# Seven block products in a second output layer, their order and sums rearranged, and a fourth buffer for arriving weights

## The reference, cut to what matters

```python
def conv_ffn(x, w_up, conv_w, conv_b, w_down):
    u = causal_dwconv(x @ w_up, conv_w, conv_b)
    g, val = jnp.split(u, 2, axis=-1)
    return (jax.nn.gelu(g) * val) @ w_down          # 512 x 2816 times 2816 x 1024
...
    m = jnp.square(jax.nn.relu(h @ mlp_w1[l])) @ mlp_w2[l]   # 512 x 4096 times 4096 x 1024
    x = x + rms_norm(m, post_mlp_g[l])              # the end of the kernel
```

## Time and profile before

| | us |
|---|---|
| median of 3 runs (lowest, highest) | 1262.27 (1262.15, 1262.39) |
| the profiled execution, whole | 1265.27 |
| its span, from first to last instruction | 1263.4 |
| PE busy | 1246.5 |
| DVE busy | 816.8 |
| ACT busy | 608.2 |

### The profile page before, as it was taken

One profiled execution on the slowest core, in us unless ns is written; L12 is line 12 of the kernel. 1 busy time (PEld: TensorE's weight loads), 2 busy tenths in 40 slices (PEclk: granted clock), 3 DMA queues, 4 the chain that ended last, 5 costly groups with the idle time before them and its releaser, 6 DMA issues.

```text
span 1263.4 us, 16035 instructions
## 1 busy us (share of the span) xinstructions
PE 1246.5 (99%) x6278; PEld 1047.0 (83%) x6278; DVE 816.8 (65%) x1179; ACT 608.2 (48%) x1022; POOL 28.9 (2%) x40
## 2 busy tenths in 40 slices
PE   9999999999999999999999999999999999899997
PEld 9877798898888888888888898778898888788785
DVE  5778878575577555555633488888574443577785
ACT  4565654254446444444522364578443422365563
POOL 0000001000000000000000000000000000000000
PEclk9999999999999999999999999999999999999999
DMA  8345445422236466545754276434473333256562
GB/s 265 136 150 200 134 134 183 145 73 67 84 118 200 167 167 156 167 163 148 209 166 164 78 176 196 134 106 149 130 200 100 101 100 99 101 183 200 166 202 98
DMA packets 53892, 186.79 MB, mean 148 GB/s; under 512 B 5781, under 2 KB 13461, under 8 KB 49465
## 3 DMA queue, kind: packets, MB, share of 16 engines
q1 hardware_dynamic: 48776, 151.82, 37.1%
q0 software_dynamic: 4608, 33.56, 10.7%
q10 hardware_dynamic: 432, 0.39, 0.1%
HBM read 177.88 MB, written 39.32 MB: 172 GB/s over the span
## 4 chain that ended last, share of the span: by engine, by line
PE 84%; DVE 3%; ACT 2%; issue 1%; DVEq 0%; ACTq 0%
PE bank L1392 16%; PE bank L1393 15%; PE bank L1394 15%; PE bank L1593 3%; PE bank L1594 3%; PE bank L1595 3%; PE bank L1533 3%; PE bank L1538 3%; PE bank L1535 3%; PE bank L1536 3%; PE bank L1534 3%; PE bank L1537 3%; PE bank L1643 1%; DVE wlo L2318 1%; PE bank L1514 1%
## 5 line engine op out<-in xcount | busy, mean ns | idle before, releaser
L1392 PE MATMUL bank<-xh,whi 128*128 128x512 f32 (+1 forms) x1136 | 413.7, 364 | 1.0 <-DVE R L2553 0.8
L1393 PE MATMUL bank<-xl,whi 128*128 128x512 f32 (+1 forms) x1136 | 409.9, 361 | 0.0
L1394 PE MATMUL bank<-xh,wlo 128*128 128x512 f32 (+1 forms) x1136 | 409.8, 361 | 0.0
L2318 DVE TENSOR_TENSOR wlo<-stage,whi 128x1024 fp32r<-128x1024 f32 (+1 forms) x246 | 296.7, 1211 | 156.2 <-ACT whi L1826 154.8
L1826 ACT CAST whi<-stage 128x1024 fp32r<-128x1024 f32 (+1 forms) x246 | 254.0, 1038 | 130.7 <-PE bank L1538 58.6
L1392 PEld LDWEIGHTS bank<-xh,whi 128*128 128x128 f32 x1136 | 214.4, 189 | 38.8 <-issue 5.5
L1394 PEld LDWEIGHTS bank<-xh,wlo 128*128 128x128 f32 x1136 | 214.4, 189 | 32.8
L1393 PEld LDWEIGHTS bank<-xl,whi 128*128 128x128 f32 x1136 | 214.5, 189 | 31.8 <-issue 0.2
L1593 PE MATMUL bank<-whi,xh 128*128 128x512 f32 x220 | 86.4, 393 | 5.6 <-issue 3.2
L1595 PE MATMUL bank<-whi,xl 128*128 128x512 f32 x220 | 86.3, 392 | 0.0
L1594 PE MATMUL bank<-wlo,xh 128*128 128x512 f32 x220 | 86.3, 392 | 0.0
(11 more groups left out here) (374 smaller groups left out, 1625.2 us busy)
## 6 DMA issues: line engine op xcount, KB each, us to landing
stage<-in_W_m SPq DMA_DIRECT2D x56, 512.0 KB, 3.6
stage<-in_W_up SPq DMA_DIRECT2D x44, 512.0 KB, 3.7
stage<-in_W_down SPq DMA_DIRECT2D x22, 512.0 KB, 3.6
stage<-in_W_in_a SPq DMA_DIRECT2D x19, 512.0 KB, 3.8
stage<-in_W_out SPq DMA_DIRECT2D x16, 512.0 KB, 4.1
sum_a<-in_W_m POOLq DMA_DIRECT2D x8, 1024.0 KB, 8.0
sum_b<-in_W_m POOLq DMA_DIRECT2D x8, 1024.0 KB, 7.4
stage<-in_W_in_b SPq DMA_DIRECT2D x10, 512.0 KB, 4.2
```

The costliest lines, as they stand in the source:

```text
L1392: e.matmul(b[:, cols], hi[:, k, :], xh[:, k, cols], start=(k == 0), stop=False)
L1393: e.matmul(b[:, cols], hi[:, k, :], xl[:, k, cols], start=False, stop=False)
L1394: last = e.matmul(b[:, cols], lo[:, k, :], xh[:, k, cols], start=False, stop=(k == 7))
L2318: e.tensor_tensor(wlo[:, plan.place[i], c], stage[:, i % NSTAGE, c], whi[:, plan.place[i], c].bitcast(F32), ALU.subtract).then_inc(S["w_lo"])
```

## The change

- **down** is now computed like m2 for the first 16 of its 22 tiles of hidden width: 4 groups, 28 products of 12 matmuls each (16 in part one, 12 in part two), and then the 6 remaining tiles as full chunks as before. The layer has 34 chunks instead of 22. The six full chunks are exactly the six that its tail takes tile by tile.
- Sums and combinations carry the layer's name (down_a to down_d, m2_a to m2_d). There are 48 DMAs on GpSimd instead of 32, one for every two chunks: 22 of them during up, none during down, the rest from the first chunk of the second mixer to chunk 23 of m1.
- The last chunk of up and of m1 signals a semaphore (half) after its first 12 matmuls. The tiles x_from 1 to 3 of the layer that follows wait for that and stand in front of the last chunk's own evaluation.
- In both layers the combination r2 of group 0 is made early, beside the first tile. In m2 the combinations r1 and r3 of group 7 are moved behind x_from 4 to 6.
- Around the change of parts: pump (the split of a chunk) now stands in front of taken; the x_from that stood there and in the next two steps come together after c21. 
- Part two takes t22, t12, r4 for every group but the first.
- ScalarE's squares of the last layer go to sq2 instead of sq, and its waits for pn_x are gone there.
- NSTAGE is 4, with the room taken from the tile more (4 tiles instead of 6; two of the r tiles of m2 now lie in gb). Two semaphores were merged to stay within their number.

The core of the diff:

```diff
-NSTAGE, NSPLIT = 3, 6
+NSTAGE, NSPLIT = 4, 6
...
-           ("xq", 8), ("xo", 8), ("up", 44), ("down", 22), ("in2_c", 4), ("in2_a", 2), ("in2_v", 2), ("in2_d", 2), ("in2_b", 10),
+           ("xq", 8), ("xo", 8), ("up", 44), ("down", 34), ("in2_c", 4), ("in2_a", 2), ("in2_v", 2), ("in2_d", 2), ("in2_b", 10),
...
-SEVEN = ([(kind, g) for g in range(8) for kind in ("r1", "r2", "t11", "r3")]
-         + [(kind, g) for g in range(8) for kind in ("t12", "r4", "t22")])
+GROUPS = {"down": 4, "m2": 8}
+SEVEN = {n: [(kind, g) for g in range(k) for kind in ("r1", "r2", "t11", "r3")]
+         + [(kind, g) for g in range(k) for kind in (("t22", "t12", "r4") if g else ("t12", "r4", "t22"))]
+         for n, k in GROUPS.items()}
+LAST_X = {"down": ("up", 2 * NF1 - 1), "m2": ("m1", NF2 - 1)}
...
         for j in self.feat("up", 2 * NF1):
+            if j == 2 * NF1 - 1:
+                self.seven_ahead("down")
             self.step("up", j // 2, j % 2)
             self.out(("up", j), "up_y", j + 1)
+            if j % 8 == 7 and j < 8 * GROUPS["down"]:
+                self.combine("down", "r1", j // 8)
+                self.combine("down", "r3", j // 8)
...
-        self.tok_full("down", NF1)
+        self.seven("down")
...
+    def seven_ahead(self, name):
+        for i in range(1, 4):
+            self.seven_x(name, i)
...
         for i in range(n - 6):
             self.need()
-            self.step("seven", i)
+            self.step("seven", name, i)
             self.used += 1
-            if i == 29:
-                self.step("taken")
-            if i == 30:
+            ready = [i + 7]
+            if i == last - 2:
+                ready = []
+                self.pump()
+                self.step("taken", name)
+            elif i == last - 1:
+                ready = []
                 for kind in ("v", "w"):
                     for t in range(2):
-                        self.combine(kind, t)
-            if i == 31:
-                self.step("seed")
+                        self.combine(name, kind, t)
+            elif i == last:
+                ready = [i + 5, i + 6, i + 7]
+                self.step("seed", name)
                 for kind in ("c22", "c21"):
                     for t in range(2):
-                        self.combine(kind, t)
+                        self.combine(name, kind, t)
             self.pump()
-            if i + 7 < n:
-                x_from(i + 7)
+            for k in ready:
+                if k < n:
+                    self.seven_x(name, k)
...
+                if (name, j) in LAST_X.values():
+                    by_weights(b, i, cols, range(4)).then_inc(S["half"])
+                    ks = range(4, 8)
...
             def last_norm():
...
-                q.wait_ge(S["pn_x"], 7)
...
-                    e.activation(sq[:, hf * 512:(hf + 1) * 512], bank_of("m2", 2 * t + hf)[:], ACT.Square,
+                    e.activation(sq2[:, hf * 512:(hf + 1) * 512], bank_of("m2", 2 * t + hf)[:], ACT.Square,
```

More of the change, by code:

```diff
@@ new lines, in seven_x, with seven_first, seven @@
+    def seven_x(self, name, i):
+        kind, g = SEVEN[name][i] if i < len(SEVEN[name]) else ("", 0)
+        if kind in ("r2", "r4") and i > 1:
+            self.combine(name, kind, g)
+        self.step("x_from", name, i)
+        self.x_split(name, i)
+    def seven_first(self, name):
+        self.step("first", name)
+        self.combine(name, "r2", 0)
+    def seven_ahead(self, name):
+        for i in range(1, 4):
+            self.seven_x(name, i)
+    def seven(self, name):
+        n, last = NK[name], 4 * GROUPS[name] - 1
@@ L1064, in seven @@
         for kind in ("r1", "r2", "t11", "r3"):
             for b in INTO[kind]:
-                self.fill("m2", b)
-        for i in range(1, 7):
-            x_from(i)
+                self.fill(name, b)
+        for i in range(4, 7):
+            self.seven_x(name, i)
+        if name == "m2":
+            self.combine("m2", "r1", 7)
+            self.combine("m2", "r3", 7)
         for i in range(n - 6):
             self.need()
-            self.step("seven", i)
+            self.step("seven", name, i)
@@ L1101, in mlp @@
         self.step("rows", "pl")
-        self.seven()
+        self.seven("m2")
         self.step("warm", 4)
@@ L1143 @@
 SEMAPHORES = (
-    ["st0", "st1", "st2"] + [f"ld_x{k}" for k in range(5)]
+    ["st0", "st1", "st2", "st3"] + [f"ld_x{k}" for k in range(5)]
     + ["ld_w0", "ld_xf", "w0_lo", "ld_xr", "ld_c", "ld_masks", "ld_bias", "ld_mem", "ld_rows",
@@ L1292, in build_program, with t_of, seven_x @@
         hid2 = tiles(reg(16, NF2 * 512), NF2)
-        rs = [tiles(more[:, g, :], 2) for g in range(6)] + [tiles(reg(92 + 2 * g, 512), 2) for g in range(2)]
+        rs = ([tiles(more[:, g, :], 2) for g in range(4)] + [tiles(reg(92 + 2 * g, 512), 2) for g in range(2)]
+              + [tiles(gb[:, 1, 512 * g:512 * g + 512], 2) for g in range(2)])
+        hidden = {"down": hid1, "m2": hid2}
         vs, ws = tiles(sq, 2), tiles(sq2, 2)
-        def t_of(which, g):
+        def t_of(name, which, g):
             i, j = int(which[1]) - 1, int(which[2]) - 1
-            return hid2[:, 4 * g + 2 * j:4 * g + 2 * j + 2, 256 * i:256 * i + 256]
-        def seven_x(i):
-            kind, g = SEVEN[i]
+            return hidden[name][:, 4 * g + 2 * j:4 * g + 2 * j + 2, 256 * i:256 * i + 256]
+        def seven_x(name, i):
+            kind, g = SEVEN[name][i]
             if kind == "r3":
-                return t_of("t21", g)
-            return t_of(kind, g) if kind[0] == "t" else rs[g]
+                return t_of(name, "t21", g)
+            return t_of(name, kind, g) if kind[0] == "t" else rs[g]
         source = {"out1": hT, "down": hid1, "out2": yT, "m2": hid2}
@@ L1591, in seven_products @@
                     c = slice(256 * j + 128 * t, 256 * j + 128 * t + 128)
-                    new, end = i < 4 and j == 0, g == 7 and j == 1
+                    new, end = i < 4 and j == 0, g == GROUPS[name] - 1 and j == 1
                     e.matmul(b[:], x[:, c], hi, start=new, stop=False, skip_group_check=True)
@@ L1848, in x_from @@
             def x_from(name, k):
-                q.wait_ge(S["mm"], CHUNK0[name] + max(0, k - 7))
+                if name in SEVEN and k < 4:
+                    q.wait_ge(S["half"], HALVES[name])
+                else:
+                    q.wait_ge(S["mm"], CHUNK0[name] + max(0, k - 7))
                 if name == "out1":
```

238 lines of the change are left out of this document (123 added, 115 removed).

## The result

The changed kernel takes 1241.96 us (median of four runs, 1241.44 to 1243.73) against 1262.33 for the kernel before in the same series (1262.15 to 1264.06). The ratio is 0.9838 (0.9821 to 0.9855), the medians are 20.4 us apart. The forecast was 20.5 off and 1241.8.

The account below looks back on a forecast made before the run. PE, busy 99% of the span, was taken to bound the kernel. Terms of 10.9 + 0.3 + 4.9 + 1.3 + 3.1 = 20.5 us took the median from 1262.27 to 1241.8, range 1238.8 to 1247.5.

Parts of the forecast that it names:

- 48 matmuls and the start of down: Down: 48 fewer matmuls at 0.226 us give 10.9 us, and the hole at its start goes, 0.3 us.
- start of m2: Start of m2: the hole goes, 3.3 us, and the clock no longer falls, 1.6 us; together 4.9 us.
- change of parts in m2: Between parts one and two of m2: PE's idle time behind v goes, 1.3 us.
- tail of m2: Tail of m2: the wait behind the last wlo goes by earlier t22 chunks, 1.2 us.
- the end: Last tile: ScalarE's squares no longer wait for VectorE; 3.1 us together with the tail's hole of 1.2.
- transfers, fourth buffer: Whole kernel: chunks and sums land in time, 0, with at most 1 us for late loads; a fourth buffer may save 0.5.
- Down has no hole of its own at the change: Down's change of parts: 0 forecast; rival, new holes in down or a rest of m2's, 1243 to 1248, chance 0.19.
- over 8: Down: a chunk's landing would have to rise from 3.6 us to over 8 for transfers to turn the sign.
- The rival that transfers starve the products: Up and down: crowded sums make chunks land late and stretch every product, for example 1279 us; slower, chance 0.03.
- the 3.0 us between profile and median of before: Whole kernel: the gap between profiled execution, 1265.27, and median, 1262.27, was assumed to stay the same.

Follow-up runs that it names:

- experiment 1: The changed kernel with down as 22 full chunks again, without its sums and early tiles: 1253.58 us, ratio 0.9924.
- experiment 9: The changed kernel with ScalarE's squares of the last layer in sq again and its waits for VectorE back: 1244.0 us, ratio 0.9851.
- experiment 10: The changed kernel with three buffers (NSTAGE 3) in place of four: 1242.04 us, ratio 0.9836.
- experiment 4: The changed kernel with the old change of parts in both layers, taken before the split and no x_from put off: 1246.62 us, ratio 0.987.
- experiment 5: The changed kernel with x_from in their old place at the change of parts, the split still before taken: 1245.15 us, ratio 0.9863.
- experiment 8: The changed kernel with the old change of parts and the old order of kinds together, in both layers: 1247.37 us, ratio 0.9882.
- Experiment 11: The changed kernel, four buffers, with m2's sums 22 to 47 started in down, one per chunk: 1248.61 us, ratio 0.9887.
- experiment 12: The changed kernel with m2's sums 22 to 47 started in down, and three buffers instead of four: 1261.04 us, ratio 0.9986.
- experiment 2: The changed kernel with tiles 1 to 3 of down and m2 no longer made before the preceding layer's last chunk is evaluated: 1247.70 us, ratio 0.9877.
- experiment 7: The changed kernel with part two as t12, r4, t22 in every group: 1243.78 us, ratio 0.9847.

## Why the prediction was right

Its terms beside what the runs showed:

| term | forecast | measured |
|---|---|---|
| 48 matmuls and the start of down | 10.9 + 0.3 | 11.24 in the traces, 11.6 by experiment 1 |
| start of m2 | 4.9 | 3.34 + 1.67 = 5.0 in the trace of before |
| change of parts in m2 | 1.3 | 1.42 + 0.09 = 1.5 |
| tail of m2 | 1.2 | 1.32 + 0.13 = 1.45 |
| the end | 1.9 | 1.87; 2.0 by experiment 9 |
| transfers, fourth buffer | 0 | 0 (experiment 10) |
| sum | 20.5 | 21.2 in the traces (0.1 of it in no term above), 20.4 between the medians |

- **The matmuls.** 48 x 0.226 us held: the whole of down is 11.24 shorter, 10.88 of it at 0.2267 each and 0.36 the hole at its start. The figure of 131 ns that I set beside it from the Trainium skill ("TensorE: Matmul & The Clock Gate", section "Back-to-back issue gap") would have made an estimated 6.3 us. The trace of after does not agree: of its 4391 matmuls of 128 by 512 columns all but one start 0.22 us or more before the next.
- **The start of down.** The hole went, by a shorter way than laid out: ScalarE began to cast tiles 1 to 3 0.8 us before the end of up (612.87) and not 2.7, because a cast of weights (611.93) stood in front. VectorE was through with them 1.2, 1.8 and 2.4 us behind the end, about as forecast (1 to 2.2), and PE needed the first at 2.7.
- **The start of m2.** Right in kind and size, hole and clock. The forecast read the clock's part from one hole of before, which happened to be at the small end: across all runs a hole of 3 to 4.4 us cost 1.67 to 2.9 us on top.
- **The change of parts.** The schedule laid out step by step is the part I trusted least, and it can be laid beside the rows. Product 29 is over at about 1163.4. Counted from there v was to be done at 4.0, w at 5.3, the seeds at 5.9, c21 at 9.0. The rows say 4.1, 5.3, 6.0 and 8.9. The size 1.3 was the row's idle time before the instruction; what counts is the distance of starts and the two matmuls behind it, and that was 1.5. The same holds for the tail (1.2 against 1.45). Both errors are in the same direction and come to 0.45 us.
- **Down has no hole of its own at the change.** That rival had most of the rest. Experiments 4, 5 and 8 show what stood behind it: without the putting-off the hole is there, 1.3 to 1.8 us in each layer, so it was a live case. Its place is right and its releaser was not: with the new kinds it is a seed.
- **The end.** VectorE was forecast to be through with the third tile 0.5 us before PE ends; the rows say 1233.73 against 1234.21. The squares now follow PE. Behind them VectorE's L2945 ends at 1235.65 and ScalarE's root at 1235.49, so an earlier root alone would bring nothing. To let VectorE read the last bank beside ScalarE's square might, and that wasn't tried.
- **Transfers.** The 0 was right. The working behind it was too easy. I took 10.9 us as what a chunk has for landing and split, and "over 8" as the landing from which it hurts. Experiment 11 makes holes with a median landing of 6.0 us. A median says little: chunks read from sums took up to 9.4 and one wait was 8.0 us. The rival that transfers starve the products was named with the right mechanism (the section "Issuing engines are not separate DMA queues" of "DMA: Bandwidth & Descriptors" in the Trainium skill, that GpSimd's DMAs run on the same 16 as SyncE's; experiments 11 and 12 agree: SyncE's chunks went from 4.1 us to 6.0 and 6.4). To come true it needed more than this change does: the sums that after leaves to the second mixer, crowded into down.

Two things in the forecast were right by luck. The first is how close it came: by the traces the change is worth 21.2 us, 0.7 more than the terms, and the ratio of the medians leaves 18 to 23, so a forecast of 20.5 against 20.4 is closer than the working was. The second: I let the 3.0 us between profile and median of before stand on both sides. They did not: after's profiled execution lies 0.4 below its median, at 1241.57 where the working gave 1244.8, and the stretch before up is 2.4 us shorter in it than in before's. The forecast was made for the median, so it changed nothing.

## What to carry over

Read each engine's queue in order and give every step the moment at which PE needs it. At m2's change of parts that gave four moments to within 0.1 us. The experiments then showed which moves were needed (tiles made ahead, x_from put off) and which was not (the split before taken). Cost a hole by the distance of starts, not by the idle time in the row, and put 1.5 to 3 us on top for the clock when it is about 3 us or more (behind 1.8 us or less the clock stayed up, and no hole between the two was seen). Give a buffer its worth only at the load it is for: the fourth was worth 0 in this kernel, and 12 us when the same sums started in down and not in the second mixer.

## What the runs showed of the hardware

- **Slow stretches behind holes.** In the two output layers a hole of 1.8 us or less never lowered the granted clock (eleven holes of 1.0 to 1.8 us in experiments 2, 4, 5, 7, 8 and in before). Each of seven of 2.95 us or more did. What was lost after it, in us, by size of hole: 2.95: 1.67; 3.34: 1.67; 3.40: 2.73; 3.82: 2.65; 4.01: 2.93; 4.37: 2.53; 9.30: 1.44. It does not follow the hole's size. It does follow the stretch of low clock: by the record of the granted clock that lasts 3.4 us behind the holes of 2.95 and 3.34, where it begins 0.85 and 1.1 us after PE has resumed, and 6.8 us at the other five, where it begins inside the hole. What is lost is, to within 0.1 us, half of the part in which PE works again, which comes in the same order to 1.71, 1.71, 2.84, 2.74, 3.04, 2.61 and 1.46. So the hole of 9.30 loses least: 3.9 of its 6.8 us at 1.2 GHz passed while PE stood. One of the short ones, from experiment 2:

```profile
620.89:624.30 3.41, 3.41 (x10) 2.64 (x9) 2.73 (x5) 1.92 (x3) 0.00 (x0) 0.50 0.80 300
```

  What PE did before each hole was the same dense work at 1.00. What sets the start and the length of the low stretch is open.
- **Late handovers.** An instruction of VectorE normally starts 0.10 us after the ScalarE instruction that it waits for. Three of 119 wlo in after start 0.45 to 0.47 us behind it, and the kernel of experiment 7 has its late ones at the same steps of the program; before has one of 122, at 583.19. It is tied to the place in the program and not to chance. What stands beside them in the traces is the transfer of instructions. The page of after has this queue, whose 8 KB transfers are rare (18 of them after 370 us):

```profile
q14 instruction: 27, 0.22, 0.1%
```

  Behind each of the 37 late wlo of all fourteen traces such a transfer starts within 0.6 to 3.3 us, and behind only 42 of the 1484 others. That the engine waits for its instructions there is a guess that no run tests.
- **The opening** varies by 2 us between executions of the same instructions, in part in PE's waits for small transfers (0.2 to 1.4 us where there is one). Terms of a microsecond can't be read from two spans without cutting at the stages.
